# The even layer's attention placed inside its input projection, and the head norm's factors by token columns

## The chip, the cores and the metric

One core of a Trainium2 chip runs the kernel. The time is device microseconds (us) from the first to the last instruction of one execution, the median of the runs.

## The reference, cut to what matters

Two layers on 256 tokens of width 1024, all float32. The change is inside the first (even) one:

```python
h = _rmsnorm(x, norm_mix_g[l]) * (1.0 + sc1) + sh1
z = h @ even_w_in[e]                       # 1024 x 4096
o_a = _hgrn2(z[..., :5 * A_WIDTH], lower_bounds[e], hgrn_norm_g[e])
q_b, k_b, v_b = jnp.split(z[..., 5 * A_WIDTH:], 3, axis=-1)
o_b = _neighbourhood_attention(q_b, k_b, v_b, na_rpb[e])   # 8 heads of 64
mixed = jnp.concatenate([o_a, o_b], axis=-1) @ even_w_out[e]
x = x + g1 * mixed
...
# inside _hgrn2, 4 heads of 128: gates f by sigmoid, k = (1 - lb) * sigmoid(-f), two scans, then
o = o_fwd + o_bwd
o = o * lax.rsqrt(jnp.mean(o * o, axis=-1, keepdims=True) + RMS_EPS) * norm_g
return o.transpose(0, 2, 1, 3).reshape(B, T, A_WIDTH) * jax.nn.silu(g)
```

The vectors `mod` (scales, shifts and gates of a layer) are one 1024 x 6144 product with a single row; the kernel sums them on DVE in tiles of 128 x 1024, each fetched from HBM.

## The kernel before, in words

**Units.** All weight matrices are streamed as 110 units of 1 MB (128 x 2048 floats). SP fetches a unit into one of four `w_raw` slots (L359), once the unit four before it has been split (the wait on `s_lo`, L353). A unit is split into two fp32r numbers, `w_hi` by ACT in two halves (`split_hi`, L565) and `w_lo` by DVE in two halves (`split_lo`, L858), with two slots of each: the split of unit n+2 waits for TensorE's last product with unit n (`w_used`). TensorE makes three products for each piece (`three`, L1296), 48 of 256 columns a unit, into one of the two `acc` banks. ACT evicts the bank to `ze` (L632, `z_evicted`) and then splits the unit after next.

**Even projection.** Units 0 to 15, in the order of the columns of `even_w_in`: q, two gates, values, output gate g of the recurrence (0 to 9), then q and k (10 to 13) and v (14, 15) of the attention. Units 6, 7, 14 and 15 are made by token, the others by feature. Beside them DVE adds ada tiles (`add_tile`, L868): tiles 0 to 19 of the layer's remaining 24 come from POOL's queue (L444), four more from SP's (L400), two buffers in all, each refilled when DVE has used it. On TensorE `turn_bias` makes the attention's bias tables between units 9 and 10 and between units 11 and 12; DVE keeps them (L996). ACT makes the recurrence's gates after units 12, 13 and 14 (L649 to L653), and POOL goes on from them in a chain (L487 to L502) to `own_k`.

**Attention.** After the last unit, eight steps of two heads and 128 queries each. A step: two score products on TensorE (L1502), bias and scale on DVE (L1033), the row maximum (L1037), exponentials on ACT (L660), reciprocal and scaling on DVE (L1042, L1046), four transposes on TensorE (`turn_even`, L1513), a copy on ACT (L672), eight output products (`out_even`, L1532), a copy on ACT (L677). The engines go through the steps in order, shifted against each other. POOL splits `w_lo` of the first two output units meanwhile (L509), and DVE adds four ada tiles.

**Recurrence.** Levels of block size 1 to 128 (`within`, `across`; L1555, L1572): DVE multiplies the four decay-weighted copies of q and k by block totals (`grow`, L324, and `next_total`, L1052), TensorE makes the products of the next level, DVE picks them by mask (L1083). Then value products (L1612).

**Head norm and output projection.** ACT copies and squares the output of two head pairs (L700, L702); TensorE makes the mean, spread over the partitions, with a 128 x 128 matrix of 1/128 (L1618); ACT takes the root of 128 x 512 (L705), DVE the reciprocal (L1117), then two multiplies (L1120, L1123). ACT and DVE split the result for the output projection. On TensorE `part_of` runs the halves of its first two units that need only the attention (k 4 to 7) around the head means, and the halves that need the recurrence (k 0 to 3) after them.

**The odd layer**, later in the same kernel, has its dilated attention inside the units of its own projection (`BESIDE`, `BREAKS` at L1300), and POOL makes a pooling mixer beside it (L531 to L540).

## Time and profile before

| | |
|---|---|
| median of 3 runs | 814.58 us (806.07 to 817.91) |
| the profiled execution, its span | 812.2 us |
| TensorE busy in it | 756.3 us (93%) |
| DVE busy | 577.9 us (71%) |
| ACT busy | 422.2 us (52%) |
| mean granted TensorE clock | 0.954 of 2.4 GHz |
| even projection, about | 39 to 135 us |
| attention of the even layer, about | 135 to 166 us |
| recurrence's levels and values | to 195 us |
| head norm and output projection | to 227 us |

A timeline shows instructions in order of time: start in us, duration in us (of one, or from the first's start to the last's end), engine, line, operation, output<-inputs, shape, count, and in brackets how long the engine was idle before and what ended that. PE is TensorE, SP the queue of SyncE. The ends of matmuls are modelled. The chain of waits is the work that ended last, followed back: start, duration, engine, tile, line, count.

### The profile page before, as it was taken

Reading aid. Unit: us, or ns where it says so; the run is one execution under the profiler, and the core shown is the slowest. Engines: PE = TensorE matmul, PEld = TensorE weight load, DVE = VectorE, ACT = ScalarE, POOL = GpSimd, SP = SyncE. Lnnn points to the kernel's source line nnn. Section 1 sums busy time; section 2 is a strip of 40 time slices with the busy share of each in tenths; the row PEclk is TensorE's granted clock in tenths of the full one; section 3 lists DMA queues with packets and bytes.
Section 4 is the critical chain, followed back from the end, with each engine's and each line's share of the span. In section 5 each row is a group of like instructions: output and inputs, shape, how many; then the busy total and the mean of one; then the engine's idle time right before and its main releaser. Section 6 shows DMA issues by size and latency. Waiting matters only on the chain.

```text
span 812.2 us, 16869 instructions
## 1 busy us (share of the span) xinstructions
PE 756.3 (93%) x6609; PEld 728.5 (90%) x6609; DVE 577.9 (71%) x787; ACT 422.2 (52%) x660; POOL 105.6 (13%) x123
## 2 busy tenths in 40 slices
PE   3799997889789999999998999999898999999997
PEld 3799996578789999999998999898798999999997
DVE  4856687996679999766547778966557788886442
ACT  4444356732366666763335555455645766666332
POOL 2201117802001010000010004500003100000001
PEclk9599999689899999999998999999998999999999
DMA  8999887511348989757673997664133877865401
GB/s 327 371 292 355 305 271 255 159 32 53 83 117 259 287 271 279 257 179 264 230 259 111 310 346 244 208 237 153 52 103 107 252 235 239 242 219 196 182 39 52
DMA packets 161392, 171.23 MB, mean 211 GB/s; under 512 B 5453, under 2 KB 142358, under 8 KB 161344
## 3 DMA queue, kind: packets, MB, share of 16 engines
q1 hardware_dynamic: 153536, 143.13, 55.7%
q0 software_dynamic: 7808, 27.43, 9.3%
q8 instruction: 33, 0.54, 0.3%
q14 instruction: 15, 0.12, 0.1%
HBM read 169.49 MB, written 1.05 MB: 210 GB/s over the span
## 4 chain that ended last, share of the span: by engine, by line
PE 74%; DVE 12%; DMA 6%; issue 4%; ACT 3%; SPq 2%; DVEq 0%; POOLq 0%; ACTq 0%
PE acc L1296 53%; PE big L1296 13%; DVE w_lo L858 4%; DMA ada_raw<-in_ada_w 4%; DMA w_raw<-in_even_w_in 2%; SPq L337 2%; DVE mod_acc L868 1%; ACT w_hi L565 1%; PE aux L1405 1%; DVE o_rms L1117 1%; PE acc L1405 1%; DVE mod_acc L1166 1%; DVE qk L324 1%; PE big L1405 1%; PE big L1555 1%
## 5 line engine op out<-in xcount | busy, mean ns | idle before, releaser
L1296 PE MATMUL acc<-h_hi,w_hi 128*128 128x256 f32 x1248 | 355.5, 285 | 14.8 <-DVE h_lo L910 5.9
L1296 PE MATMUL acc<-h_lo,w_hi 128*128 128x256 f32 x1248 | 351.6, 282 | 0.0
L1296 PE MATMUL acc<-h_hi,w_lo 128*128 128x256 f32 x1248 | 351.3, 281 | 0.0
L858 DVE TENSOR_TENSOR w_lo<-w_raw,w_hi 128x1024 fp32r<-128x1024 f32 x216 | 263.9, 1246 | 95.4 <-ACT w_hi L565 95.4
L565 ACT ACTIVATE w_hi<-w_raw 128x1024 fp32r<-128x1024 f32 x220 | 224.6, 1050 | 93.5 <-PE acc L1296 87.8
L1296 PEld LDWEIGHTS acc<-h_hi,w_hi 128*128 128x128 f32 x1248 | 241.0, 193 | 18.2 <-issue 12.6
L1296 PEld LDWEIGHTS acc<-h_lo,w_hi 128*128 128x128 f32 x1248 | 239.5, 192 | 0.7 <-issue 0.5
L1296 PEld LDWEIGHTS acc<-h_hi,w_lo 128*128 128x128 f32 x1248 | 239.1, 192 | 0.0
L1296 PE MATMUL big<-hid_hi,w_hi 128*128 (+1 forms) x308 | 86.2, 280 | 0.0
L1296 PE MATMUL big<-hid_lo,w_hi 128*128 (+1 forms) x308 | 85.7, 278 | 0.0
L1296 PE MATMUL big<-hid_hi,w_lo 128*128 (+1 forms) x308 | 85.7, 278 | 0.0
L868 DVE SCALAR_TENSOR_TENSOR mod_acc<-ada_raw,cact,mod_acc 128x1024 f32<-128x1024 f32 x48 | 61.6, 1284 | 12.5 <-DMA ada_raw<-in_ada_w 12.4
L734 ACT ACTIVATE conv<-acc,vecs 128x256 f32<-128x256 f32 x44 | 24.9, 566 | 68.7 <-PE acc L1296 68.7
L1296 PEld LDWEIGHTS big<-hid_hi,w_hi 128*128 128x128 f32 x308 | 58.4, 190 | 0.5 <-issue 0.4
L444 POOL DMA_DIRECT2D ada_raw<-in_ada_w x44 | 23.7, 539 | 268.0 <-DVE mod_acc L868 268.0
L1296 PEld LDWEIGHTS big<-hid_lo,w_hi 128*128 128x128 f32 x308 | 57.8, 188 | 0.0
L1296 PEld LDWEIGHTS big<-hid_hi,w_lo 128*128 128x128 f32 x308 | 57.8, 188 | 0.0
L1182 DVE SCALAR_TENSOR_TENSOR conv<-acc,vecs,conv 128x255 f32<-128x255 f32 x44 | 21.2, 483 | 37.7 <-ACT conv L734 37.7
L1296 PE MATMUL acc<-w_hi,h_hi 128*128 128x256 f32 x144 | 40.5, 281 | 1.6 <-DVE w_lo L858 1.6
L1296 PE MATMUL acc<-w_hi,h_lo 128*128 128x256 f32 x144 | 40.0, 277 | 0.0
L1296 PE MATMUL acc<-w_lo,h_hi 128*128 128x256 f32 x144 | 40.0, 277 | 0.0
L632 ACT ACTIVATE ze<-acc 128x512 f32 (+1 forms) x16 | 9.6, 598 | 46.8 <-PE acc L1296 46.8
(246 smaller groups left out, 948.5 us busy)
## 6 DMA issues: line engine op xcount, KB each, us to landing
w_raw<-in_ffn_w_up SPq DMA_DIRECT2D x88, 512.0 KB, 4.9
ada_raw<-in_ada_w POOLq DMA_DIRECT2D x52, 512.0 KB, 5.4
w_raw<-in_ffn_w_down SPq DMA_DIRECT2D x44, 512.0 KB, 3.9
w_raw<-in_odd_w_in SPq DMA_DIRECT2D x40, 512.0 KB, 5.6
w_raw<-in_even_w_in SPq DMA_DIRECT2D x32, 512.0 KB, 8.6
ada_raw<-in_ada_w SPq DMA_DIRECT2D x24, 512.0 KB, 4.7
ada_first<-in_ada_w SPq DMA_DIRECT2D x12, 512.0 KB, 12.9
w_raw<-in_even_w_out SPq DMA_DIRECT2D x8, 512.0 KB, 5.1
```

Source lines behind the costliest of these rows:

```text
L324: return eng.tensor_tensor(to, to, total.unsqueeze(3).to_broadcast([P, 2, half // (2 * h), h]), ALU.mult)
L337: sp.dma_start(ada_first[k][:, cols], ada_w[0, k * P:(k + 1) * P, cols]).then_inc(landed[k], 16)
L444: pool.dma_start(ada_raw[:, slot, :], src.rearrange("k p n -> p (k n)")).then_inc(ada_landed[slot], 16)
L565: nc.scalar.activation(w_hi[:, n % SPLIT, part], w_raw[:, n % RAW, part], ACT.Copy).then_inc(s_hi, 1)
L632: nc.scalar.activation(to, acc[:, (n - first) % 2, :], ACT.Copy, scale=scale).then_inc(z_evicted, 1)
L734: nc.scalar.activation(conv[:, a, :], acc[:, a, 0:T], ACT.Identity, bias=vecs[:, bass.ds(i * 4 + (V_CB + l * FT + u), 1)], scale=vecs[:, b ...
L858: dve.tensor_tensor(w_lo[:, n % SPLIT, part], w_raw[:, n % RAW, part], w_hi[:, n % SPLIT, part].bitcast(F32), ALU.subtract).then_inc(s_lo, 1)
L868: dve.scalar_tensor_tensor(out=sums, in0=ada_raw[:, slot, :], scalar=cact[:, bass.ds(k, 1)], in1=sums, op0=ALU.mult, op1=ALU.add).then_inc ...
L1117: link(dve.reciprocal(o_rms[:, part], o_rms[:, part]))
L1182: dve.scalar_tensor_tensor(out=conv[:, a, 1:T], in0=acc[:, a, 0:T - 1], scalar=tap(0), in1=conv[:, a, 1:T], op0=ALU.mult, op1=ALU.add).the ...
L1296: ins = pe.matmul(dst, lhsT, rhs, start=start and n == 0, stop=stop and n == 2, skip_group_check=True)
L1405: ins = pe.matmul(bank[0:count, 0:P], pick, mod_acc[:, blocks[g] * P:(blocks[g] + 1) * P], start=g == 0, stop=g == count - 1, skip_group_c ...
```

## The change

- **Order of units.** The projection runs units 10 to 15 first, then 2 to 5, 0, 1, 6 to 9 (`EVEN`). From here on, "unit 6" of the changed kernel means the seventh in time. All loops are written out.
- **Attention in steps.** Eleven calls of `neighbours` (s = 0 to 10) on TensorE, two inside each of units 6 to 10 (after 5 and 10 of the 16 groups of three products) and one inside unit 11: scores of step s, output of s-3, turn of s-2. DVE and ACT have the same steps in their iteration of the unit before, which is the one that splits the weights for the unit after. Within DVE's step the reciprocal and scaling of step s-1 come first. The attention's output goes to `aux`.
- **w_lo shared.** For units 2 to 11 (`HALVED`) DVE makes the first half and POOL the second, in two pieces of 128 x 512.
- **Ada tiles.** All 24 are added in the projection (`EVEN_TILES`: one in each of the first five iterations, two in the next nine, one in the fifteenth); 16 come from POOL's queue, each behind POOL's pieces, eight from SP's, two ahead of each load of an output unit.
- **Bias tables** are turned before units 4 and 5; their rows are fetched after the load of unit 4.
- **Gates.** ACT makes the four sigmoids in its iteration 9 and the silu of q in iteration 11; silu of g follows the last eviction. POOL's chain to `own_k` begins after its last piece and its last tile; the `w_lo` of the first two output units follows `own_k`.
- **Head norm.** No copy to `work`: ACT squares, TensorE sums each 128 tokens into one column (four products with one column), ACT and DVE take root and reciprocal of 4 columns, TensorE spreads them again (`head_spread`), and DVE multiplies o by norm_g and silu(g) from PSUM and then by the spread factors.

The core of the diff:

```diff
-ADA1_POOL = 20
+ADA1_POOL = 16
+EVEN_TILES = (1, 1, 1, 1, 1, 2, 2, 2, 2, 2, 2, 2, 2, 2, 1, 0)
...
+NA_AT, NA_STEPS = 6, 11
+HALVED = tuple(range(2, 12))
+def na_steps(p):
+    return tuple(s for s in (2 * (p - NA_AT), 2 * (p - NA_AT) + 1) if 0 <= s < NA_STEPS)
...
                 if not (isinstance(i, int) and 4 * i + n < RAW):
                     sp.wait_ge(s_lo, i * 8 + 2 * (n - RAW + 1))
+                    if isinstance(i, int) and n - RAW - EI in HALVED:
+                        sp.wait_ge(s_lo_pool, HALVED.index(n - RAW - EI) + 1)
...
-            project(even_w_in[0], EI, N_EI, skip=8)
-            project(even_w_out[0], EO, N_EO)
-            for tile in range(ADA1_POOL, ADA2 - ADA1):
-                sp.wait_ge(ada_used, ADA1 + tile - 1)
-                k, q, slot = tile % KT, tile // KT, tile % 2
-                sp.dma_start(ada_raw[:, slot, :], ada_w[0, k * P:(k + 1) * P, 2048 + q * 1024:3072 + q * 1024]).then_inc(
-                    rest_landed[slot], 16)
+            tile = ADA1_POOL
+            for p, u in enumerate(EVEN):
+                load(0, EI + p, columns(even_w_in[0])[:, :, u * 256:(u + 1) * 256])
+                if p == 4:
+                    sp.dma_start(consts[:, C_HMEAN:C_DIST], consts_in[:, C_HMEAN:C_DIST]).then_inc(s_const, 16)
+                    bias_rows(0)
...
+            def first_tiles(first, last):
+                for tile in range(first, min(last, ADA1_POOL)):
+                    tile_in(0, tile % KT, 2048 + tile // KT * 1024, tile % 2, 0, (ADA1 + tile) // 2)
+            def lo_pieces(n, half):
+                pool.wait_ge(s_hi, 2 * n + half + 1)
+                for piece in (2 * half, 2 * half + 1):
+                    part = slice(piece * UNIT // 4, (piece + 1) * UNIT // 4)
+                    ins = pool.tensor_tensor(w_lo[:, n % SPLIT, part], w_raw[:, n % RAW, part],
+                                             w_hi[:, n % SPLIT, part].bitcast(F32), ALU.subtract)
+                return ins
+            first_tiles(0, 2)
+            for p in HALVED:
+                lo_pieces(EI + p, 1).then_inc(s_lo_pool, 1)
+                used = sum(EVEN_TILES[:p - 2])
+                first_tiles(2 + used, 2 + used + EVEN_TILES[p - 2])
             pool.wait_ge(lb_ready, 1)
...
                     cols = slice(h * T, (h + 1) * T)
                     ins = pool.tensor_tensor(qk[:, 1 + d, cols], qT[:, cols], fT[1 - d][:, cols], ALU.mult)
-            ins.then_inc(gates_ready, 1)
-            pool.wait_ge(z_evicted, N_EI)
+            link(ins)
...
+            pool.wait_ge(s_lo, 2 * EO)
             for n in (EO, EO + 1):
                 for half in (0, 1):
...
+                    lo_pieces(n, half).then_inc(s_lo, 1)
             pool.wait_ge(mod_gathered, 2)
...
+            def attend_even(s):
+                r = s - 3
+                if 0 <= r < PAIRS:
+                    act.wait_ge(attended, 2 * r + 2)
+                    nc.scalar.activation(work[:, 4 + r // 2, (r % 2) * P:(r % 2 + 1) * P], aux[:, r % 2, 0:P],
+                                         ACT.Copy).then_inc(out_placed, 1)
+                r = s - 2
                 if 0 <= r < PAIRS:
                     act.wait_ge(turned, 2 * r + 2)
                     if r >= 2:
                         act.wait_ge(attended, 2 * r - 2)
                     nc.scalar.activation(npt[:, r % 2].rearrange("p b k -> p (b k)"), aux[:, r % 2, :], ACT.Copy).then_inc(
                         probs_kept, 2)
-                r = p - 2
-                if r >= 0:
-                    act.wait_ge(attended, 2 * r + 2)
-                    nc.scalar.activation(work[:, 4 + r // 2, (r % 2) * P:(r % 2 + 1) * P], acc[:, r % 2, 0:P],
-                                         ACT.Copy).then_inc(out_placed, 1)
-            for p in range(PAIRS + 1):
-                attend_even(p)
+                if s < PAIRS:
+                    act.wait_ge(shifted, 2 * s + 2)
+                    for b in (0, 1):
+                        nc.scalar.activation(big[:, 2 + s % 2, b * T:(b + 1) * T], big[:, 2 + s % 2, b * T:(b + 1) * T], ACT.Exp,
+                                             bias=pstat[:, s % 4, 0, b:b + 1], accum_out=pstat[:, s % 4, 1, b:b + 1]).then_inc(
+                            exp_done, 1)
+            for p, u in enumerate(EVEN):
+                n = EI + p
+                act.wait_ge(w_used, n + 1)
+                nc.scalar.activation(ze[:, u, :], acc[:, p % 2, :], ACT.Copy).then_inc(z_evicted, 1)
+                split_hi(0, n + SPLIT)
+                if p == 2:
+                    act.wait_ge(lb_diff, 1)
+                    nc.scalar.activation(lbt[:, 1, :], lbt[:, 0, :], ACT.Exp).then_inc(lb_exp, 1)
+                for s in na_steps(p + 1):
+                    attend_even(s)
+                if p == 9:
+                    act.wait_ge(bias_kept, NA_HEADS)
+                    act.wait_ge(z_evicted, 10)
+                    for d in (0, 1):
+                        nc.scalar.activation(qk[:, 3 * d, :], fT[d], ACT.Sigmoid, scale=-1.0).then_inc(gate_act, 1)
+                        act.wait_ge(gate_act, 2 * d + 1)
+                        nc.scalar.activation(fT[d], fT[d], ACT.Sigmoid).then_inc(gate_act, 1)
+                if p == 11:
+                    act.wait_ge(z_evicted, 12)
+                    nc.scalar.activation(qT, qT, ACT.Silu).then_inc(gate_act, 1)
+            act.wait_ge(z_evicted, N_EI)
+            nc.scalar.activation(gT, gT, ACT.Silu).then_inc(gate_act, 1)
             act.wait_ge(gla_done, 3)
...
-            attend_even(PAIRS + 1)
-            nc.scalar.activation(gT, gT, ACT.Silu).then_inc(gate_act, 1)
...
             for b in (0, 1):
                 act.wait_ge(gla_out, b + 1)
-                nc.scalar.activation(work[:, 2 * b:2 * b + 2, :].rearrange("p k t -> p (k t)"), big[:, b, :],
-                                     ACT.Copy).then_inc(gla_sq, 1)
                 nc.scalar.activation(o_sq[:, b * 512:(b + 1) * 512], big[:, b, :], ACT.Square).then_inc(gla_sq, 1)
             for b in (0, 1):
                 act.wait_ge(gla_mean, b + 1)
-                nc.scalar.activation(o_rms[:, b * 512:(b + 1) * 512], aux[:, b, :], ACT.Sqrt,
+                nc.scalar.activation(head_col[:, b, :], aux[:, b, 0:4], ACT.Sqrt,
                                      bias=consts[:, C_EPS:C_EPS + 1]).then_inc(gla_rms, 1)
...
-            for p in range(PAIRS):
-                attend_even(p)
-                if p < 4:
-                    add_first(ADA1_POOL + p)
+            tiles = iter(range(ADA2 - ADA1))
+            for p in range(N_EI):
+                if p + SPLIT < N_EI:
+                    if p + SPLIT in HALVED:
+                        split_lo(0, EI + p + SPLIT, (0,), each=2)
+                    else:
+                        split_lo(0, EI + p + SPLIT)
+                if p == 3:
+                    dve.wait_ge(s_const, 16)
+                    keep_bias(0, 4)
+                if p == 4:
+                    keep_bias(4, NA_HEADS)
+                    dve.wait_ge(lb_exp, 1)
...
+                    dve.tensor_scalar(lbt[:, 5, :], lbt[:, 0, :], -1.0, 1.0, ALU.mult, ALU.add).then_inc(lb_ready, 1)
+                left = EVEN_TILES[p]
+                for s in na_steps(p + 1):
+                    if s <= PAIRS:
+                        attend_even(s)
+                    if left:
+                        add_first(next(tiles))
+                        left -= 1
+                for _ in range(left):
+                    add_first(next(tiles))
+            dve.wait_ge(z_evicted, N_EI)
             dve.wait_ge(own_ready, 1)
             next_total(0)
-            attend_even(PAIRS)
...
             keep_mods(1, 24, acc[:, 1])
+            def head_work(b):
+                return work[:, 2 * b:2 * b + 2, :].rearrange("p k t -> p (k t)")
+            def head_gated(b):
+                dve.wait_ge(gate_act, 6)
+                dve.wait_ge(gla_sq, b + 1)
+                dve.scalar_tensor_tensor(out=head_work(b), in0=big[:, b, :], scalar=vecs[:, V_HG:V_HG + 1],
+                                         in1=gT[:, b * 512:(b + 1) * 512], op0=ALU.mult, op1=ALU.mult).then_inc(gla_gated, 1)
+            def head_rstd(b):
+                dve.wait_ge(gla_rms, b + 1)
+                dve.reciprocal(head_col[:, b, :], head_col[:, b, :]).then_inc(gla_rstd, 1)
+            def head_scaled(b):
+                dve.wait_ge(gla_gated, b + 1)
+                dve.wait_ge(gla_spread, b + 1)
+                dve.tensor_tensor(head_work(b), head_work(b), big[:, 2 + b, :], ALU.mult).then_inc(gla_normed, 1)
+            head_gated(0)
+            head_rstd(0)
+            head_gated(1)
+            head_rstd(1)
             take_mods(1, 0, 16, 24, acc[:, 1])
+            head_scaled(0)
+            mixed_lo(MIX_AT[0] + 2, slice(0, 2))
+            head_scaled(1)
             make_gain(1, 0, 32, V_NFFN)
-            def head_pair(b):
-                part = slice(b * 512, (b + 1) * 512)
...
-                dve.wait_ge(gla_rms, b + 1)
-                link(dve.reciprocal(o_rms[:, part], o_rms[:, part]))
-                if b:
-                    mixed_lo(MIX_AT[0] + 2, slice(0, 2))
-                link(dve.scalar_tensor_tensor(out=o, in0=o, scalar=vecs[:, V_HG:V_HG + 1], in1=o_rms[:, part],
-                                              op0=ALU.mult, op1=ALU.mult))
-                dve.wait_ge(gate_act, 6)
-                dve.tensor_tensor(o, o, gT[:, part], ALU.mult).then_inc(gla_normed, 1)
-            head_pair(0)
...
                 if r >= 2:
-                    pe.wait_ge(probs_kept, 2 * r - 2)
+                    pe.wait_ge(out_placed, r - 1)
...
             def out_even(r):
                 if r == 0:
-                    pe.wait_ge(z_evicted, N_EI)
-                if r >= 2:
-                    pe.wait_ge(out_placed, r - 1)
-                if r in (PAIRS - 4, PAIRS - 3):
-                    pe.wait_ge(own_ready, 1)
-                    pe.wait_ge(gates_ready, 1)
-                    within(1, r - PAIRS + 4).then_inc(gla_done, 1)
+                    pe.wait_ge(z_evicted, NA_AT)
                 pe.wait_ge(probs_kept, 2 * r + 2)
...
-                        ins = pe.matmul(acc[b * DH:(b + 1) * DH, r % 2, 0:P], v, npt[:, r % 2, b, kt * P:(kt + 1) * P],
+                        ins = pe.matmul(aux[b * DH:(b + 1) * DH, r % 2, 0:P], v, npt[:, r % 2, b, kt * P:(kt + 1) * P],
...
-                    within(0, 0)
-                    within(0, 1).then_inc(gla_done, 1)
+            def neighbours(s):
+                if s < PAIRS:
+                    score_even(s)
+                if 0 <= s - 3 < PAIRS:
+                    out_even(s - 3)
+                if 0 <= s - 2 < PAIRS:
+                    turn_even(s - 2)
+            for p, u in enumerate(EVEN):
+                if p == 4:
+                    pe.wait_ge(s_const, 16)
+                    pe.wait_ge(s_bias, 16 * 2)
+                    turn_bias(0, 4)
+                if p == 5:
+                    turn_bias(4, NA_HEADS)
+                if p == NA_AT:
+                    pe.wait_ge(bias_kept, NA_HEADS)
+                n, beside = EI + p, tuple(partial(neighbours, s) for s in na_steps(p))
+                split_ready(0, 2, n)
+                if p in HALVED:
+                    pe.wait_ge(s_lo_pool, HALVED.index(p) + 1)
                 if p >= 2:
-                    out_even(p - 2)
-            out_even(PAIRS - 1)
+                    pe.wait_ge(z_evicted, p - 1)
+                if u in (6, 7, 14, 15):
+                    token_major(n, p % 2, beside=beside)
+                else:
+                    feature_major(n, p % 2, NORM_AT[0] if p == 0 else None, beside=beside)
+            pe.wait_ge(z_evicted, N_EI)
+            pe.wait_ge(out_placed, PAIRS)
+            pe.wait_ge(own_ready, 1)
+            for c in (0, 1):
+                within(1, c).then_inc(gla_done, 1)
+            within(0, 0)
+            within(0, 1).then_inc(gla_done, 1)
...
             def head_mean(b):
-                pe.wait_ge(gla_sq, 2 * b + 2)
-                pe.matmul(aux[:, b, :], hmean_w, o_sq[:, b * 512:(b + 1) * 512], start=True, stop=True).then_inc(
-                    gla_mean, 1)
+                pe.wait_ge(gla_sq, b + 1)
+                for j in range(4):
+                    at0 = b * 512 + j * P
+                    ins = pe.matmul(aux[:, b, j:j + 1], o_sq[:, at0:at0 + P], hmean_w[:, 0:1], start=j == 0, stop=True,
+                                    skip_group_check=True)
+                ins.then_inc(gla_mean, 1)
+            def head_spread(b):
+                pe.wait_ge(gla_rstd, b + 1)
+                for j in range(4):
+                    ins = pe.matmul(big[:, 2 + b, j * P:(j + 1) * P], head_col[:, b, j:j + 1].to_broadcast([P, P]), ident,
+                                    start=j == 0, stop=True, skip_group_check=True)
+                ins.then_inc(gla_spread, 1)
...
-            head_mean(0)
+            head_mean(1)
             part_of(EO, 0, (4, 5), MIX_AT[0] + 1, first=True)
-            head_mean(1)
+            head_spread(0)
+            head_spread(1)
             part_of(EO, 0, (6, 7), MIX_AT[0] + 1)
             pe.wait_ge(mod_ready, 2)
             part_of(EO + 1, 1, (4, 5, 6, 7), MIX_AT[0] + 1, first=True)
```

## Rows read from the trace of the kernel before

**Rows 1.** Timeline of ACT in the even projection.

```profile
44.92 0.60 ACT L632 ACTIVATE ze<-acc 128x512 f32 x1 [2.82 <-PE acc L1296]
45.42 2.00 ACT L565 ACTIVATE w_hi<-w_raw 128x1024 fp32r<-128x1024 f32 x2
50.35 0.60 ACT L632 ACTIVATE ze<-acc 128x512 f32 x1 [2.94 <-PE acc L1296]
```

**Rows 2.** Windows: us, busy PE, PEld, DVE, ACT, POOL; PEclk, DMA, GB/s.

```profile
135.00:162.00 27.00, 19.90 (x150) 12.06 (x147) 24.13 (x50) 18.59 (x50) 24.43 (x23) 0.68 0.50 161
```

**Rows 3.** The chain of waits, 157 to 245 us: start, duration, what.

```profile
166.81 0.93 DVE qk L324 x2
...
175.87 3.65 PE big L1555 x64
...
190.98 3.65 PE big L1612 x16
194.80 1.07 PE aux L1618 x2
...
201.48 3.27 DVE o_rms L1117
...
205.62 7.24 PE acc L1296 x36
...
227.54 1.69 PE aux L1355 x16
```

**Rows 4.** Timeline of TensorE: bias turn, score, turn, and a norm's spread.

```profile
94.01 2.74 PE L1482 MATMUL big<-nflip,consts 128*128 128x384 f32 x8
...
157.41 0.70 PE L1502 MATMUL big<-ze 64*128 64x256 f32 x4
...
158.25 0.66 PE L1513 MATMUL aux<-consts,ns 128*128 128x128 f32 x4
...
229.77 0.71 PE L1363 MATMUL aux<-consts,rcol 128*128 128x128 f32 x4 [0.55 <-DVE rcol L890]
```

**Rows 5.** Timelines of DVE and POOL, w_lo and the gate chain.

```profile
126.30 1.22 DVE L858 TENSOR_TENSOR w_lo<-w_raw,w_hi 128x1024 fp32r<-128x1024 f32 x1
...
142.89 1.40 POOL L497 TENSOR_TENSOR qk<-ze 128x256 f32<-128x256 f32 x2
...
148.66 10.86 POOL L509 TENSOR_TENSOR w_lo<-w_raw,w_hi 128x512 fp32r<-128x512 f32 x8
...
152.09 2.50 POOL L509 TENSOR_TENSOR w_lo<-w_raw,w_hi 128x512 fp32r<-128x512 f32 x2
```

**Rows 6.** Timelines of DVE and POOL in the odd layer's projection.

```profile
507.26 2.09 DVE L858 TENSOR_TENSOR w_lo<-w_raw,w_hi 128x1024 fp32r<-128x1024 f32 x1
...
508.35 1.60 POOL L536 TENSOR_TENSOR s<-s 128x256 f32<-128x256 f32 x1
...
509.27 1.75 DVE L858 TENSOR_TENSOR w_lo<-w_raw,w_hi 128x1024 fp32r<-128x1024 f32 x1
```

**Rows 7.** Timelines of ACT and DVE in the attention.

```profile
137.01 0.45 ACT L660 ACTIVATE big<-big,pstat 128x256 f32<-128x256 f32 x1 [0.34 <-DVE pstat L1037]
...
137.84 0.20 ACT L660 ACTIVATION_READ_ACCUMULATOR big<-big,pstat 128x1 f32 x1
...
138.54 0.76 DVE L1033 SCALAR_TENSOR_TENSOR big<-big,nbias 128x256 f32<-128x256 f32 x2
...
140.99 1.35 DVE L868 SCALAR_TENSOR_TENSOR mod_acc<-ada_raw,cact,mod_acc 128x1024 f32<-128x1024 f32 x1
```

**Rows 8.** Timeline of ACT at the gates.

```profile
118.48 1.28 ACT L649 ACT_TABLE_LOAD   x1
120.88 1.06 ACT L649 ACTIVATE qk<-ze 128x1024 f32<-128x1024 f32 x1 [1.12 <-DVE nbias L996]
```

**Rows 9.** The page's DMA issues: count, KB of each, us to landing.

```profile
ada_raw<-in_ada_w POOLq DMA_DIRECT2D x52, 512.0 KB, 5.4
...
ada_raw<-in_ada_w SPq DMA_DIRECT2D x24, 512.0 KB, 4.7
```

159 lines of the change are left out of this document (40 added, 119 removed).

## The prediction, made before the changed kernel was run

> **What bounds the kernel now.** I read first the ACT timeline of the even projection. A unit's 48 products take 5.44 us: ACT evicts one at 44.92 and the next at 50.35, and between them splits the weights of the unit after next (two halves, 2.0 us) [rows 1]. So TensorE is the bound there, at 2.4 GHz. From 135 to 162 us, the attention of the even layer, it is not: the windows view shows it 19.9 of 27 us busy at a granted clock of 0.68, so most of this stretch runs at 1.2 GHz, while DVE is busy 24.1 us [rows 2]. Then come the gated recurrence's levels and the head norm. The chain of waits shows in which order these set the end: the second level's multiplies on DVE start at 166.81; the head mean's product ends at 195.9, the second 3.3 us reciprocal ends at 204.75, and the output projection's first-half products run 205.62 to 212.86, 36 of them at 0.20 us each, thus at 1.2 GHz, against 0.113 in the projection [rows 3]. I use 166.81 and 212.86 as the two marks that the change has to move. Everything after 212.9 is the same code.
>
> **What the change buys on TensorE.** The attention's products go into units 6 to 11, so its 27 us should shrink to their own time. At 2.4 GHz a step has a score (0.7 us), a turn (0.66) [rows 4] and an output that I count like the turn; their ends overlap the next product, so 1.65 us each, 13.2 for eight. Projection with attention would be 16 x 5.44 + two bias turns of 2.6 (the row's 2.74 less its tail [rows 4]) + 13.2 = 105.4 us from 39.5 (44.92 less one unit), an end at 144.9. The start of the second level follows a projection end by 5.2: eviction 0.6, first total 1.25, four multiplies 2.45, second total 0.7, two starts 0.2. That gives 150.1, and 16.7 us are gained, if no other engine is slower. This is the lower bound of the cost (zero stall). The next three parts ask whether DVE, ACT and POOL keep up.
>
> **Units 0 to 5: POOL's half.** DVE now subtracts one half of w_lo (1.22 us) and POOL the other in two pieces of 1.23 [rows 5]. From a unit's end E: ACT evicts (0.5), second half of w_hi at E+2.5. The rows of the odd layer show what happens when POOL and DVE both read SBUF: a w_lo half that normally takes 1.22 took 2.09 and 1.75, each exactly until POOL's instruction was over plus 1.1, and POOL's 1.60 in between likewise waited for DVE; they take turns, whole instruction by whole instruction [rows 6]. So: DVE half until E+2.8, POOL piece to 4.0, DVE's ada tile (1.28) to 5.3, POOL piece to 6.5. The unit after next can start at E+6.7, where E+5.2 was wanted. It costs 1.4 us every second unit; units 4 and 5 are covered by the bias turns in front of them. One stall counts: E of unit 5 is 44.92 + 5 x 5.44 + 5.2 + 1.4 = 78.8. Bound below: 0, if the tile lands later than the pieces.
>
> The Trainium skill ("SBUF — State Buffer", section "SBUF: two separate sides") calls the pair of ports that DVE and GpSimd share an exclusive lock, held for the whole instruction by DVE work with two SBUF inputs; the sum by it is the one here, and without it the 1.4 us and the larger terms below would be nil.
>
> **Units 6 to 9: a loop of DVE and ACT, without TensorE.** DVE's step is add, reduce, reciprocal, two scalings: 138.54 to 140.99, 2.45 us; the tile behind it 1.27 [rows 7]. ACT's two exponentials end 1.03 after they start (137.01 to 138.04) [rows 7]. ACT works in order: the exponential of the second step stands before the eviction and w_hi of the next unit, and DVE's next iteration begins by waiting for that w_hi half. The loop: exponentials 1.05, eviction 0.5, w_hi half 1.05, w_lo half 1.25, scalings of the last step 1.0, add and reduce 1.45, tile 1.25, scalings 1.0, add and reduce 1.45 = 10.0 us for each two steps. TensorE needs 5.44 + 3.3 = 8.7, so it stalls about 1.3 a unit at the second score. First reduce pair done at 78.8 + 9.0 (one tile waits 1.0 for POOL's piece) = 87.8, that of steps 6 and 7 at 117.8. Two more tiles a unit come from POOL's queue, in which each issue stands behind the two pieces; they land in 5.4 us of a 10 us loop and cost nothing.
>
> **Units 10 to 15.** After 117.8: exponentials, eviction, w_hi, w_lo half and scalings 4.9; turn and copy of the last probabilities 1.3; then ACT has the gates in line, a table load 1.28 and four of 1.06 [rows 8], to 129.6. Behind them in its queue stand the eviction of unit 10 and w_hi of unit 12 (2.5), then w_lo (2.8 with POOL between): unit 12 starts at 135.1, where TensorE was ready at 132.5, and ends at 140.5. From here DVE has both halves again and two tiles a unit, four instructions of about 1.2, and POOL is in its gate chain: 20 instructions of about 0.7 to 0.75 once free (two in 1.40 [rows 5]), each taking its turn. Four of each are 7.6 to 7.8 us a unit against 5.44. With the waits that TensorE still covers I get 7.4: unit 15 ends at 140.5 + 3 x 7.4 = 162.7. The SP queue now has each pair of tiles ahead of an output weight; a tile there lands 4.7 us after its issue [rows 9], and with use and issue a slot turns in 6.3, within the 7.4, but the last tile, number 23, lands 2 us after unit 15 and DVE takes it before the recurrence. Bounds: no lock at all, 5.6 to 6.5 a unit (end at 155); every instruction blocked fully, 8 (165).
>
> **Into the levels.** own_k is ready on POOL at about 163.8, and POOL goes on to the eight w_lo pieces of the first two output units, 10.86 us [rows 5]. Before, these ran at 148.7 to 159.5 beside the attention, whose DVE work reads PSUM and was not slowed. Now they run beside the last tile, first total, four multiplies and second total, all with two SBUF inputs, in front of my mark. Taking turns: 8 x 1.2 + tile 1.15 + total 1.15 + 5 x 0.6 + issue 0.2 = 15.1. The second level starts at 178.8 against 166.81: 12.0 later. Bound below, if these multiplies are not blocked: 170. So the attention stretch does not pay: 27 us vanish, 39 return.
>
> **Head norm.** Removed: two copies to work (0.5 each in ACT's queue), two products over 512 columns, two square roots of 0.7, two reciprocals of 3.35, one multiply of the pair. Added: four one-column products a pair (eight took 1.69, so 0.84 [rows 3]), a root and a reciprocal of 4 columns (about 0.2 each), four spreads (two took 0.71 [rows 4], so 1.1 to 1.3), and a gated multiply (0.76) off the path. Counted with the levels' end where it was (194.63): means to 196.5, 12 products to 197.9, spreads to 199.9, 12 + 24 products to 204.0; scaling, h_hi and h_lo of the first pair are done at 201.0 and of the second at 203.1, hidden under them; 24 and 12 products more complete the first unit at 208.1. Mark before: 212.86. Gain 4.8, of which 3.2 is that TensorE never pauses and keeps 2.4 GHz (36 products at 0.113, not 0.20). Bounds 3 and 6.5.
>
> **Sum.** 812.2 + 12.0 - 4.8 = 819.4 us for a profiled execution; the median of the runs shown is 814.58, 2.4 above it, so 821.8, say 821.
>
> **The rivals.** *TensorE stays the bound*: DVE and ACT keep pace; 16.7 + 4.8 gained, 793. Against it stands the loop of 10.0 over 8.7. Chance 0.06. *The loop, but no turns of the port*: E of unit 15 at 155.1, last tile at 158.4, mark at 162.8; gain 4.0 + 4.8, so 805.8. For it: in the even layer's gates a DVE tile of 1.35 ran beside POOL almost without loss [rows 7]; against: rows 6. Chance 0.2. *Turns, but POOL's pieces mostly over before DVE wants the port* (own_k ready 5 us earlier, or the multiplies not blocked): mark 7 lower, 814. Chance 0.17. *The forecast*, +3 to +11: 0.47. *The clock*, the rival on the slow side: the levels begin with about 10 us in which TensorE does little, and it then runs the levels, values and head products at 1.2 GHz as it did in [rows 2, 3]. The chain before has 18.8 us of such products between 175.9 and 194.6 [rows 3], some of them slow already (I count 4.8); 14 more give 833 to 835. It decides if the clock from 180 to 205 reads under 0.6. Chance 0.1. That the head norm's form changes nothing is not likely enough to count: the two reciprocals stand alone in the chain.
>
> **How the numbers follow.** 2% is about what a measurement can tell from no change: under 798.3 or over 830.9. Faster 0.06 (the first), slower 0.1 (the clock), same 0.84. The range goes from the second rival less its scatter, 804, to 832. The forecast alone: 815 to 826.
>
> **What would show it.** Evictions of units 6 to 9 some 10 us apart (8.7: TensorE bound); ACT idle before the exponentials on DVE's reduce; w_lo and tile instructions of DVE at 1.9 to 2.5 us instead of 1.2 where POOL works; units 13 to 15 at 7.4; eight L509-type pieces on POOL beside the first multiplies, these 1.8 instead of 0.6; the head norm's output products without a gap at clock 1.00. Wrong if DVE's instructions keep their 1.2, or if unit 15 ends before 156.

## The result, and the profile after

The changed kernel took 814.22 us (median of 20 runs, 809.82 to 824.55); the kernel before, in the runs beside it, 811.88 (20 runs, 805.01 to 821.22). The ratio is 1.0072 with a 95% interval of 1.0049 to 1.0095: 4.0 to 7.7 us slower, well within 2%. The ratios, here and below, leave out executions that are more than 1.5% above the fastest of the same kernel; the two plain medians lie only 2.3 us apart. A second series gave 817.95 against 811.25, ratio 1.008 [1.0038, 1.0122]. The forecast was 821 and +6.4 us against the median that was shown.

The profiled execution has a span of 822.9 us, the repeat 818.1, before 812.2. These spans are not compared below, since some 7 us of them are explained by nothing in the code (last section). Behind the first output unit the first profile has 606.3 us, the repeat 601.3 and the kernel before 599.3: five of the seven microseconds belong to the one execution, and the other two stay unexplained. Marks inside the even layer are compared instead: the evictions of the units, the start of the second level, and the eviction of the first output unit.

The page of the kernel after, busy time by engine. DVE is busy for 576.3 us and POOL for 145.7; below it the group of POOL's pieces of low halves, 28 of them with a mean of 1.66 us, where eight of before took 10.86 in all [rows 5]:

```profile
PE 761.9 (93%) x6637; PEld 736.6 (90%) x6637; DVE 576.3 (70%) x777; ACT 417.2 (51%) x656; POOL 145.7 (18%) x139
...
L513 POOL TENSOR_TENSOR w_lo<-w_raw,w_hi 128x512 fp32r<-128x512 f32 x28 | 45.9, 1661 | 28.1 <-ACT w_hi L600 28.1
```

**Where the attention went.** The windows view, from 135 to 162 us, where TensorE was busy 19.9 us at a granted clock of 0.68 before [rows 2]:

```profile
135.00:162.00 27.00, 23.08 (x186) 22.87 (x185) 21.06 (x14) 10.17 (x12) 25.59 (x18) 0.94 0.77 258
```

TensorE now has 23.08 us here at 0.94, since units 13 to 15 of the projection stand where the attention stood. So the change does what it says; the projection ends later instead. Timeline of ACT, kernel after: first eviction (unit 0), then those of units 5, 6, 7 and 8.

```profile
44.42 0.60 ACT L686 ACTIVATE ze<-acc 128x512 f32<-128x512 f32 x1 [3.26 <-PE acc L1319]
...
78.63 0.60 ACT L686 ACTIVATE ze<-acc 128x512 f32<-128x512 f32 x1 [5.54 <-PE acc L1319]
...
88.37 0.59 ACT L686 ACTIVATE ze<-acc 128x512 f32<-128x512 f32 x1
...
99.84 0.60 ACT L686 ACTIVATE ze<-acc 128x512 f32<-128x512 f32 x1 [1.46 <-PE acc L1319]
...
109.76 0.60 ACT L686 ACTIVATE ze<-acc 128x512 f32<-128x512 f32 x1
```

Unit 9 follows at 119.67, 9.91 behind unit 8; unit 15, the last, at 162.75. Unit 7 took 11.5, which is the one place where the clock bites. Windows of TensorE alone (us, busy, granted clock, DMA share, GB/s), before and behind the second score of unit 7, kernel after:

```profile
88.00:93.00 5.00, 2.48 (x23) 0.95 0.72 244
93.00:100.00 7.00, 7.00 (x38) 0.55 0.66 225
```

In the first five microseconds TensorE works for half the time, waiting for DVE's add; then it is granted 0.55, the lower of its two levels (1.2 GHz) for most of the window, and the score that lasts 0.70 in [rows 4] takes 1.23. This dip is not fixed to the kernel: in the run with the output pieces late (below) TensorE is busy for the same 2.48 of 5 us, is granted 1.00 behind it, and unit 7 takes 9.91. It does not set the end of the projection either: the last eviction is 118.1 us behind the first there, and 118.3 and 118.2 in the two profiles of the changed kernel, both with the dip.

**Turns between DVE and POOL.** Timelines of DVE and POOL in the light units, then where the levels begin, kernel after:

```profile
47.25 2.32 DVE L888 SCALAR_TENSOR_TENSOR mod_acc<-ada_raw,cact,mod_acc 128x1024 f32<-128x1024 f32 x1
...
47.00 3.69 POOL L513 TENSOR_TENSOR w_lo<-w_raw,w_hi 128x512 fp32r<-128x512 f32 x2 [8.83 <-ACT w_hi L600]
```

```profile
160.19 15.09 POOL L513 TENSOR_TENSOR w_lo<-w_raw,w_hi 128x512 fp32r<-128x512 f32 x8
...
163.47 2.31 DVE L1037 TENSOR_TENSOR tot<-ze 128x1024 f32<-128x1024 f32 x1
165.81 6.67 DVE L336 TENSOR_TENSOR qk<-qk,ze 128x512 f32<-128x512 f32 x4
172.41 1.75 DVE L1037 TENSOR_TENSOR tot<-tot 128x512 f32<-128x512 f32 x1
174.19 3.44 DVE L336 TENSOR_TENSOR qk<-qk,tot 128x512 f32<-128x512 f32 x4
```

A tile takes 2.32 instead of 1.28 and two pieces 3.69 instead of 2.50 [rows 5]. So DVE's tile takes nearly twice its time, and POOL's pair one and a half times. The first total takes 2.31, four multiplies 6.67 (2.49 before), and the eight pieces 15.09, where [rows 5] has 10.86. The second level starts at 174.19 against 166.81 [rows 3].

**Head norm.** Chain of waits, kernel after, from the values' products to the first output unit:

```profile
199.23 3.65 PE big L1638 x16
202.88 0.79 PE aux L1647 x8
...
203.83 0.98 PE aux L1647 x8
204.81 1.49 PE acc L1319 x12
206.30 1.78 PE big L1655 x16
208.09 8.50 PE acc L1319 x72
216.60 1.07 ACT w_hi L600
```

From the values' end at 202.88 to the end of the first output unit at 216.6 it is TensorE on end: 13.7 us. Before, the same way is 194.63 to 212.86, 18.2 [rows 3]: 4.5 us gained. The window from 203 to 217 has a granted clock of 1.00.

### The profile page after: what moved, and what is told of

Its sections match the earlier page's. It is cut to its first block, busy times and chain, and to the rows that moved or that the text cites. A ratio compares the mean times of both kernels' runs of the same rounds, so it can differ in the third digit from the quotient of the medians.

```text
span 822.9 us, 16743 instructions
## 1 busy us (share of the span) xinstructions
PE 761.9 (93%) x6637; PEld 736.6 (90%) x6637; DVE 576.3 (70%) x777; ACT 417.2 (51%) x656; POOL 145.7 (18%) x139
## 4 chain that ended last, share of the span: by engine, by line
PE 74%; DVE 13%; ACT 4%; issue 4%; DMA 3%; SPq 2%; DVEq 0%; ACTq 0%
PE acc L1319 52%; PE big L1319 13%; DVE w_lo L878 5%; DMA w_raw<-in_even_w_in 2%; ACT w_hi L600 2%; DVE mod_acc L888 2%; DVE qk L336 2%; SPq L349 1%; DMA ada_raw<-in_ada_w 1%; PE aux L1428 1%; PE big L1560 1%; DVE mod_acc L1189 1%; PE big L1428 1%; PE big L1502 1%; DVE big L1027 1%
## 5 line engine op out<-in xcount | busy, mean ns | idle before, releaser
L878 DVE TENSOR_TENSOR w_lo<-w_raw,w_hi 128x1024 fp32r<-128x1024 f32 x206 | 254.8, 1258 | 110.9 <-ACT w_hi L600 110.9
L1319 PEld LDWEIGHTS acc<-h_lo,w_hi 128*128 128x128 f32 x1248 | 242.6, 194 | 0.0
L888 DVE SCALAR_TENSOR_TENSOR mod_acc<-ada_raw,cact,mod_acc 128x1024 f32<-128x1024 f32 x48 | 69.1, 1439 | 6.7 <-DMA ada_raw<-in_ada_w 6.6
L467 POOL DMA_DIRECT2D ada_raw<-in_ada_w x40 | 21.7, 543 | 208.2 <-DVE mod_acc L888 208.2
L513 POOL TENSOR_TENSOR w_lo<-w_raw,w_hi 128x512 fp32r<-128x512 f32 x28 | 45.9, 1661 | 28.1 <-ACT w_hi L600 28.1
```

The lines of the kernel that those rows point to most:

```text
L467: pool.dma_start(ada_raw[:, slot, :], src.rearrange("k p n -> p (k n)")).then_inc(ada_landed[slot], 16)
L513: ins = pool.tensor_tensor(w_lo[:, n % SPLIT, part], w_raw[:, n % RAW, part], w_hi[:, n % SPLIT, part].bitcast(F32), ALU.subtract)
L878: dve.tensor_tensor(w_lo[:, n % SPLIT, part], w_raw[:, n % RAW, part], w_hi[:, n % SPLIT, part].bitcast(F32), ALU.subtract).then_inc(s_lo, ...
L888: dve.scalar_tensor_tensor(out=sums, in0=ada_raw[:, slot, :], scalar=cact[:, bass.ds(k, 1)], in1=sums, op0=ALU.mult, op1=ALU.add).then_inc ...
L1319: ins = pe.matmul(dst, lhsT, rhs, start=start and n == 0, stop=stop and n == 2, skip_group_check=True)
```

## The experiments

All evictions, marks and gaps below are from ACT's and DVE's timelines of the profiled execution, the end of the first output unit from the chain of waits; ratios are to the kernel before beside each run. The marks lead to this table (us; "first eviction" shows how much of a shift is only an earlier start):

| kernel | first eviction | unit 5 | gap, units 8 and 9 | unit 15 | second level | first output unit | ratio, 95% |
|---|---|---|---|---|---|---|---|
| before | 44.92 | 72.11 | none | attention after it | 166.81 | 212.9 | 1 |
| changed | 44.42 | 78.63 | 9.91 | 162.75 | 174.19 | 216.6 | 1.0072 [1.0049, 1.0095] |
| changed, repeated | 44.38 | 78.17 | 9.91 | 162.54 | 175.22 | 216.8 | 1.008 [1.0038, 1.0122] |
| head norm alone | 43.70 | 70.89 | none | before's order | 165.57 | 207.1 | 0.9963 [0.9917, 1.0009] |
| the same, repeated | 45.24 | 72.43 | none | before's order | 168.22 | 209.8 | 0.995 [0.9919, 0.9981] |
| attention alone | 44.27 | 78.07 | 9.91 | 160.96 | 174.01 | 219.8 | 1.0108 [1.0042, 1.0174] |
| step before the low half | 44.39 | 78.19 | 10.55 | 165.51 | 177.67 | 219.1 | 1.0106 [1.0041, 1.0171] |
| add before scaling | 43.75 | 77.54 | 8.92 | 157.78 | 169.87 | 211.3 | 1.0006 [0.996, 1.0051] |
| pieces without reading | 45.04 | 78.84 | 9.91 | 161.53 | 167.72 | 209.3 | 0.9954 [0.9918, 0.9989] |
| halves from unit 6 | 44.65 | 77.23 | 9.92 | 159.88 | 172.99 | 214.5 | 1.005 [1.0004, 1.0097] |
| output pieces late | 43.66 | 77.66 | 9.91 | 161.76 | 166.81 | 208.2 | 0.9964 [0.9915, 1.0013] |
| two orders | 44.85 | 78.65 | 8.94 | 157.71 | 163.37 | 204.5 | 0.9912 [0.9875, 0.995] |
| all orders | 45.23 | 77.81 | 8.93 | 157.95 | 165.72 | 207.3 | 0.9927 [0.9888, 0.9965] |

How far one profile can be trusted: the second level lies 129.8 us behind the first eviction in one profile of the changed kernel and 130.8 in the other, and 121.9 and 123.0 in the two of the head norm alone. So a shift of about 1 us at that mark between two single profiles shows nothing; the way from it to the first output unit is steadier (41.5 in both profiles of the head norm alone).

**The changed kernel again, and its two parts apart.** The edits are whole parts of the diff: only the head norm of the change, in the kernel before, or everything but it.

> The changed kernel once more, for an undisturbed profile. My theory (a DVE-ACT loop of 10 us in units 6 to 9, DVE and POOL taking turns at SBUF in units 10 to 15 and in the first levels, head norm 4.5 us shorter): ratio to the kernel before 1.005 to 1.010; last eviction of the projection at 162.8 us, start of the second level's multiplies at 174, first output unit done at 216.6. If the extra 7 us after 216.6 in the first profile belong to the change, they are here again (span 822); if they are that execution's own, the span is about 816.

> The kernel before with the new head norm only, attention and projection untouched. My theory: everything to the end of the value products (194.6) stays, the first output unit is done 4.5 us earlier, at 208.3, ratio 0.994 to 0.9955. Rival (the head norm gives nothing, since the extra products on TensorE and their waits eat it): 208.3 not reached, ratio 0.999 to 1.001.

> The changed projection and attention with the old head norm. My theory: second level's multiplies at 174 as in the changed kernel, then the old head norm: first output unit done at 221, ratio 1.010 to 1.014. Rival (the attention part is neutral and the loss comes from the head norm): 1.000 to 1.004.

From the second level to the first output unit: 46.1 us before, 41.55 in both runs with the head norm alone, 45.8 with the attention alone, 41.5 in the repeat of the whole. So the head norm gives 4.5 us with the attention where it was and 4.3 with it moved. The moved attention costs 7.2 us at the second level in the run that has it alone (7.4 and 8.4 in the two profiles of the whole). The parts add within the scatter of the marks: 7.2 - 4.5 is +2.7, and the whole shows +3.7 and +3.9 at the first output unit. As ratios the parts are -0.4% and +1.1%, the whole +0.7 to +0.8%.

**The step ahead of the low half.** I thought the loop between DVE and ACT would open if DVE did the first step before it waited for w_hi.

```
-                if p + SPLIT < N_EI:
+                late = len(na_steps(p + 1)) == 2 and p + SPLIT in HALVED
+                if p + SPLIT < N_EI and not late:
...
                     if s <= PAIRS:
                         attend_even(s)
+                    if late and s % 2 == 0:
+                        split_lo(0, EI + p + SPLIT, (0,), each=2)
```

> The changed kernel with one order turned on DVE: in the five iterations with two steps of attention, DVE does the first step before its half of w_lo, not after it. My theory (the loop exponentials, eviction, w_hi half, w_lo half, scalings sets 9.9 us): w_lo leaves the loop, evictions of units 7 to 9 come 8.7 to 8.9 us apart, the last eviction is 4 to 5 us earlier (158), ratio to the kernel before 1.000 to 1.003. Rival (TensorE's own products and waits set the 9.9): the evictions stay 9.9 apart and the time that of the changed kernel.

Slower: 10.55 us a unit. Timelines of DVE and POOL of this kernel say why:

```profile
102.11 2.30 DVE L878 TENSOR_TENSOR w_lo<-w_raw,w_hi 128x1024 fp32r<-128x1024 f32 x1
104.34 2.31 DVE L888 SCALAR_TENSOR_TENSOR mod_acc<-ada_raw,cact,mod_acc 128x1024 f32<-128x1024 f32 x1
...
102.07 3.50 POOL L513 TENSOR_TENSOR w_lo<-w_raw,w_hi 128x512 fp32r<-128x512 f32 x2 [1.50 <-ACT w_hi L600]
```

Put later, DVE's half (1.23 elsewhere) meets POOL's two pieces, and so does the tile behind it. DVE no longer idles for w_hi, but its own sum is two steps of 2.45, two tiles of 1.25, one half of 1.2 and 2.1 for turns, 10.7. In the order of the change, DVE's half and the pieces are in different times, because the pieces wait for the second half of w_hi. I had expected 8.7 to 8.9. The run does not refute the loop, but this order costs more on DVE than it saves.

**Add before scaling.** The other way to open the loop: inside a step, DVE adds and takes the maximum before it scales the step before (as the kernel before did), so that the exponential runs beside the add.

```
 (attend_even, step p)
-  wait for the exponential of p - 1; reciprocal; two scalings of p - 1
   two adds of p; maximum of p
+  wait for the exponential of p - 1; reciprocal; two scalings of p - 1
```

> As the changed kernel, but inside a step of the attention VectorE adds the bias and takes the maximum of the new step first and only then takes the reciprocal and scales the step before, as the kernel before did. My theory: in the changed order VectorE waits for ScalarE's exponential, then scales, then adds, so that one loop through both engines holds add, exponential and scaling twice per unit (evictions 9.9 us apart in units 7 to 9); with the add first, VectorE works while the exponential runs, and the units come at TensorE's 8.7 to 9.0 us, the last eviction about 3.5 us earlier than the 162.54 of the repeated changed kernel, near 159. Rival: VectorE's own work and its turns with GpSimd's pieces bound the units, as in the run with the step ahead of the low half (10.55 us apart), and the evictions stay 9.9 to 10.5 us apart, the last at 162 to 165. The total: 814 to 815 by the theory, 818 or more by the rival.

The units come 8.92 to 8.93 us apart and the last eviction is at 157.78 instead of 162.54. The chain of waits shows the loop in the kernel after: from 99.87 to 123.54 it has no piece of TensorE. It goes from DVE's maximum to ACT's exponentials, the eviction and w_hi, and back to DVE:

```profile
108.12 0.70 DVE pstat L1031
...
109.87 0.49 ACT ze L686
110.36 0.95 ACT w_hi L600
```

DVE's timeline, by the low half that opens a unit; first the kernel after, then the kernel with this order (and late pieces, below):

```profile
101.49 1.23 DVE L878 TENSOR_TENSOR w_lo<-w_raw,w_hi 128x1024 fp32r<-128x1024 f32 x1 [2.97 <-ACT w_hi L600]
...
111.40 1.23 DVE L878 TENSOR_TENSOR w_lo<-w_raw,w_hi 128x1024 fp32r<-128x1024 f32 x1 [1.40 <-ACT w_hi L600]
```

```profile
89.05 1.23 DVE L879 TENSOR_TENSOR w_lo<-w_raw,w_hi 128x1024 fp32r<-128x1024 f32 x1 [0.41 <-ACT w_hi L601]
...
97.98 1.23 DVE L879 TENSOR_TENSOR w_lo<-w_raw,w_hi 128x1024 fp32r<-128x1024 f32 x1 [0.41 <-ACT w_hi L601]
```

DVE waited 1.40 us of 9.91 for ACT's w_hi, and now 0.41 of 8.93. The swap took one reciprocal with its scalings, 1.0 us, out of the loop: DVE now does them while ACT works on the exponentials and w_hi. The loop of the two engines is still there at 8.93, near DVE's own sum of 1.2 + 2 x (2.45 + 1.25) = 8.6. But TensorE is now as tight. The chain of waits of this run is TensorE alone from 91.67 to 118.35; here from one score to the same score a unit later:

```profile
96.08 0.63 PE big L1513 x4
...
97.89 1.72 PE acc L1319 x15
...
105.18 0.63 PE big L1513 x4
```

That is 9.10 us a unit, where I had counted 8.7, and between the evictions at 95.22 and 104.15 TensorE is busy for all of the 8.93 us, at a granted clock of 1.00. The evictions can come 8.93 apart for a few units because TensorE has done unit 7 some 0.8 us before ACT evicts it, and this lead shrinks from unit to unit. So by these numbers a still shorter loop would gain nothing in these units. The second level is at 169.87, 5.35 us before the repeat, of which 0.6 is an earlier start.

**Pieces that read nothing.** GpSimd writes zeros instead of subtracting, for the eight pieces of output units 0 and 1.

```
-                    lo_pieces(n, half).then_inc(s_lo, 1)
+                    pool.wait_ge(s_hi, 2 * n + half + 1)
+                    for piece in (2 * half, 2 * half + 1): ins = pool.memset(<the piece>, 0.0)
+                    ins.then_inc(s_lo, 1)
```

> As the changed kernel, but GpSimd's eight pieces of the low half for output units 0 and 1 are zeros that it writes without reading anything, so the low parts of the first two output units' weights are left out of the result. My theory: VectorE's first total (2.31 us) and first four multiplies (6.67 us) are long because they take turns at the on-chip memory with GpSimd's pieces; with nothing to read, the total takes about 1.2 us and the multiplies 2.5 us, and the second level of the attention starts near 170 instead of 174 to 175. Rival: the price does not hang on what GpSimd reads, or the second level waits for something else: 174 to 175 as before.

Timelines of POOL and DVE of this kernel:

```profile
163.13 1.95 POOL L549 MEMSET w_lo<- 128x512 f32 x4 [1.87 <-ACT w_hi L604]
...
163.33 1.22 DVE L1041 TENSOR_TENSOR tot<-ze 128x1024 f32<-128x1024 f32 x1
164.59 2.50 DVE L336 TENSOR_TENSOR qk<-qk,ze 128x512 f32<-128x512 f32 x4
167.00 0.68 DVE L1041 TENSOR_TENSOR tot<-tot 128x512 f32<-128x512 f32 x1
167.72 2.50 DVE L336 TENSOR_TENSOR qk<-qk,tot 128x512 f32<-128x512 f32 x4
```

DVE is back to 1.22, 2.50 and 0.68, even beside four memsets of POOL. With the total starting where it started in the kernel after (163.47), the second level is at 167.72: 6.5 us of the 7.4 by which the kernel after was late here are gone with POOL's reading. (This run also took away most of POOL's time, 3.9 us instead of 15.1, so it alone doesn't say whether the reading or the length counts; that the memsets from 163.13 on left the total at 1.22 speaks for the reading.) By the Trainium skill ("SBUF — State Buffer", section "SBUF: two separate sides") DVE work with two inputs in SBUF takes the lock "only against a GpSimd op that reads SBUF". The rows agree: the total takes 1.22 us beside the memsets and 2.31 beside the subtractions.

**Halves from unit 6.**

```
-HALVED = tuple(range(2, 12))
+HALVED = tuple(range(6, 12))
```

> As the changed kernel, but VectorE makes both low halves of units 2 to 5 and GpSimd only those of units 6 to 11. My theory: GpSimd's halves in the light units slow VectorE's tiles from 1.28 to 2.3 us and hold back the units there; without them the tiles take 1.28 us, and the eviction of unit 5 comes 1.2 to 1.8 us earlier (76.8 to 77.4 instead of 78.2 to 78.6), the last at 161 instead of 162.5. Rival: VectorE then has 1.2 us more per unit of its own, and the unit of 5.44 us on TensorE is missed anyway: unit 5 at 78.2 or later.

DVE's timeline of this kernel, in the second unit:

```profile
51.67 2.36 DVE L879 TENSOR_TENSOR w_lo<-w_raw,w_hi 128x1024 fp32r<-128x1024 f32 x2 [1.81 <-ACT w_hi L601]
53.95 1.28 DVE L889 SCALAR_TENSOR_TENSOR mod_acc<-ada_raw,cact,mod_acc 128x1024 f32<-128x1024 f32 x1
```

DVE idles 1.81 before it and has both halves and the tile done by 55.2, where turns with POOL took it to 54.96 in the kernel after, with POOL at work until 56.12. From the first eviction to that of unit 5 it is 32.6 us instead of the 33.8 of the repeat (32.6 again in the run with all orders, which has the same edit). The stall in the light units is 1.2 us and was POOL's doing: a half given to POOL there saves DVE nothing. The time of the run did not show it (1.005).

**Output pieces late.**

```
             pool.wait_ge(s_lo, 2 * EO)
+            pool.wait_ge(att_ready, 1)
             for n in (EO, EO + 1):
```

> As the changed kernel, but GpSimd starts its eight pieces of the low half for output units 0 and 1 only when the attention's values are ready. My theory: the first total and the multiplies run undisturbed, the second level starts near 170 instead of 174 to 175, and the pieces run beside the score and value products; the first output unit comes near 212 instead of 216.8, the total near 813. Rival: the pieces, later by some 10 us, hold back the first output unit or collide with the second level's own VectorE work, and the first output unit stays at 216 or later.

DVE's and POOL's timelines of this kernel:

```profile
162.39 1.22 DVE L1038 TENSOR_TENSOR tot<-ze 128x1024 f32<-128x1024 f32 x1 [0.25 <-ACT ze L687]
163.67 2.50 DVE L336 TENSOR_TENSOR qk<-qk,ze 128x512 f32<-128x512 f32 x4
...
166.81 2.50 DVE L336 TENSOR_TENSOR qk<-qk,tot 128x512 f32<-128x512 f32 x4
...
190.15 10.89 POOL L513 TENSOR_TENSOR w_lo<-w_raw,w_hi 128x512 fp32r<-128x512 f32 x8 [32.16 <-DVE att L1115]
```

Better than I expected: the second level at 166.81, where it was before the change, and the first output unit at 208.2. (The equality is chance, since this run starts 1.3 us before that one.) Against the repeat, and with 0.7 us taken off for the earlier start, one added wait gives back 7.8 us at the first output unit. The eight pieces have 32 us in which POOL is idle anyway, and take 10.89 there, their undisturbed time.

**Together, beside the head norm alone.** The first run joins the last wait and the add before scaling. The second adds the halves from unit 6 and moves two tiles:

```
-EVEN_TILES = (1, 1, 1, 1, 1, 2, 2, 2, 2, 2, 2, 2, 2, 2, 1, 0)
+EVEN_TILES = (1, 1, 1, 1, 1, 2, 2, 2, 2, 2, 2, 2, 1, 1, 2, 1)
```

> As the changed kernel, with two orders altered at once: inside a step VectorE adds and takes the maximum before it scales the step before, and GpSimd's eight pieces for output units 0 and 1 wait until the attention's values are ready. My theory, from the two runs that altered one of them: evictions 8.9 us apart in units 7 to 9, last eviction near 157.8, first total 1.2 us from about 159, second level near 163.5 (before: 166.81), first output unit near 205 (before: 212.88), and a time 0.7 to 0.9% under the kernel before, 804 to 806. Rival: the two gains are one and the same slack, and the second level comes no earlier than with the late pieces alone (166.8), the first output unit near 208, the time 808.

> As the run with the two orders, and besides VectorE makes both low halves of units 2 to 5, and of the tiles of the mean's sums one each (not two) is added in units 12 and 13 and one in unit 15, so that VectorE doesn't wait for a tile to land before the low half of unit 14. My theory: the light units end 1.2 to 1.7 us earlier, TensorE's wait of 4.3 us before unit 14 shrinks to under 2, the second level starts at 159 to 161 and the first output unit comes at 200 to 203, the time 800 to 803. Rival: the gates' chain on GpSimd (own_k ready at 154.6 in the run with the add first) or the tiles that now come later set the second level, which stays at 163 or later, and the time at 804 to 806.

> The head norm of the change alone, in the kernel before, once more, beside the two runs with altered orders. From the first such run: ratio 0.996 to the kernel before, first output unit 207 to 208, from the second level's start to it 41.5 us. If the attention placed inside the projection is worth anything in its best order, the runs with altered orders are faster than this one by 3 us or more; if it is worth nothing even so, they are level with it.

The two orders' gains add, as expected: second level 163.37, first output unit 204.5, 805.95 us, ratio 0.9912. By the ratio it is the fastest kernel tried, 0.9% under the kernel before, with its interval clear of 1 (by the plain medians, 805.95 against 810.77, it is 0.6%). The first output unit is 12.3 us earlier than in the repeat of the changed kernel, whose plan it shares. Beside it the head norm alone is at 807.0 and 0.995 in the same series; I had asked for 3 us or more between them; it is 1.1 by the medians and 3.1 by the ratios, and the intervals overlap, so the step from one to the other is not shown by the times. By the marks it is 5.3 us at the first output unit, 4.9 without the different start (3.8 against the first profile of the head norm alone).

The second did not do what I expected. DVE's timeline of all orders:

```profile
160.13 1.28 DVE L890 SCALAR_TENSOR_TENSOR mod_acc<-ada_raw,cact,mod_acc 128x1024 f32<-128x1024 f32 x1 [3.27 <-DMA ada_raw<-in_ada_w]
161.33 1.22 DVE L1039 TENSOR_TENSOR tot<-ze 128x1024 f32<-128x1024 f32 x1
```

The last tile lands at 160.13, after the last eviction, and DVE takes it ahead of the total: the second level is 2.35 us later than with the two orders alone. The wait of 3.4 us before unit 14's low half stayed too; the tile that lands late there is the second one of unit 11, whose number I had left at two, so this edit missed its place by one unit. And the place was the wrong one to begin with. Chain of waits of the run with the two orders:

```profile
132.95 7.29 DMA ada_raw<-in_ada_w
140.33 1.28 DVE mod_acc L889
141.66 3.43 DVE w_lo L879 x2
...
153.49 4.19 DMA ada_raw<-in_ada_w
...
158.98 1.23 DVE tot L1038
160.23 2.50 DVE qk L336 x4
```

The tiles' own landing, two slots in turn, is now what the total waits for, so a tile pushed back pushes the levels back. To take the last tile behind the total would be the next edit; it was not run.

## Why the prediction was right, point by point

- **Units 0 to 5.** Foretold: one stall of 1.4 us from turns, unit 5 at 78.8. It was 78.63, with a tile at 2.32 and a pair of pieces at 3.69; with POOL's halves taken out the stretch is 1.2 shorter. Shown.
- **Units 6 to 9.** Foretold 10.0 us a unit from a loop of DVE and ACT, not TensorE's 8.7. It was 9.91 in units 8 and 9, the chain of waits goes round DVE and ACT there without TensorE, and an order within the step shortened the loop by what it took out of it (8.93). Shown. TensorE's own sum was counted too low: 9.10 a unit by the chain of the run with the add first, with 1.8 us for a step instead of 1.65. And its pause of 1.3 a unit at the second score is not in the kernel after (0.15 us, at 114.34): it had fallen behind in unit 7, which took 11.5, at a clock of 0.55 after a half idle window. That was not foretold. Where unit 7 had no dip (output pieces late), TensorE pauses 0.75 a unit there. The clock rival looked at 180 to 205 us, where the reading was 0.91 (0.85 in the repeat), far from its 0.6.
- **Units 10 to 15.** Unit 15 foretold at 162.7, with 7.4 a unit; it came at 162.75 and 162.54. But the single units do not carry 7.4: they ended at 140.38, 146.03, 157.31 and 162.75, so 5.65, 11.3 and 5.4. The sum (22.4 against 22.2) is right, the picture of an even slowing is not. The 11.3 is a wait for the low half, which stands behind a tile that lands 3.5 us late (the same tile is waited for 3.2 to 4.0 us in the other runs with the attention moved). Its transfer took 7.02 us by the chain of waits, where I had counted 4.7. So this agreement is half luck; in the two runs with the attention alone and with pieces that read nothing, the last eviction is 1.5 to 1.8 us nearer to the first.
- **Into the levels.** The step that was mis-sized. Foretold: own_k ready at 163.8, then turns for 15.1, second level +12.0. Measured: own_k ready at 160.19, then 14.0 us to 174.19, +7.4. So 3.6 us of the 4.6 are POOL's gate chain, which I gave too long; it took 28.2 us of work (6.01, 6.03, 11.47 and 4.67) from 130.64. The other 1.0 I put down to the pieces that were over before DVE began its total at 163.47, which by the chain of waits stood behind the last tile (landed at 162.0), not behind own_k. That is the third rival in small, and the mark came two thirds of the way to its 171.8.
- **Head norm.** Foretold a gain of 4.8, measured 4.5 from the values' end in the kernel after, and 4.5 from the second level on in the repeat and in both runs with the head norm alone (in the kernel after only 3.7 by that way, because the second level's first multiplies still took 3.44 for four beside POOL); TensorE without a gap from the values' end and at 1.00.
- **The sum.** Foretold +7.2 at the marks; measured +3.7 (repeat +3.9). The ratios say +5.8 us (4.0 to 7.7) and in the repeat +6.5, at the forecast of +6.4; the plain medians beside each other say +2.3. Between 3.8 and 6 lies nothing in the profile that I could name; it is about the width of the intervals. That the ratio meets the +6.4 is therefore partly luck: what the marks show is about half of the +7.2. The median of 814.22 is 6.8 under the 821: 2.7 of that is the kernel before, 811.88 beside it rather than the 814.58 shown, and most of the rest the 3.5 at the marks. It lies in the wide range, 0.8 below the forecast's own (815 to 826), and on the 814 of the third rival.
- **The TensorE-bound rival, 793,** fell as argued. Even in the best order the last eviction is at 157.71, where the bare sum had 144.9. Of these 12.8 us the units 0 to 5 make 1.4 (78.65 against 44.85 + 5 x 5.44 + 5.2), units 6 to 9 make 0.6 (35.55 against 4 x 5.44 + 13.2), and the six units behind unit 9, with the gates and the tiles, 10.9 (43.51 against 6 x 5.44). So that stretch, not the loop I had looked at first, is where TensorE's gain is lost; no run here opened it.
- **The rival without turns, 805.8,** is refuted as a reading of this kernel by the tiles of 2.32 and by the total of 2.31. That the run with two orders came to 805.95 does not speak for it: there the turns in front of the second level are gone, but those in the projection remain, and the loop is another.

## What to carry to other kernels

Moving work under a busy engine moves every wait that it had with it: cost the loop that it forms with the two other engines in order (here 9.9 against TensorE's 9.1), and then look for work inside the moved step that can be done while the other engine has the result in hand; one swap was worth 1 us a unit. Work on POOL that reads memory is not free filler beside DVE: two streams of 1.2 us instructions took turns, DVE's took nearly twice their time and POOL's 1.4 to 1.5 times, so place such pieces where DVE works on other operands or idles, even if it looks later than needed. Where a first part gains and a second loses, run each alone; here 4.5 us of gain lay under 7 to 8 of loss, and the repair of the loss was a wait of one line.
